# Two blocks of a network on one core: an attention's scale factors turned in halves, a chunk's turns in another order, and a product in quarters

## The reference

```python
def _rwkv7_step(S, inp):
    r, w, k, v, kk, b = inp
    sa = jnp.einsum('bhvk,bhk->bhv', S, kk)
    S = S * w[:, :, None, :] - sa[..., None] * b[:, :, None, :] + v[..., None] * k[:, :, None, :]
    return S, jnp.einsum('bhvk,bhk->bhv', S, r)

# attention, grouped and neighbourhood alike
s = jnp.einsum('bqgrd,bsgd->bgrqs', qi, keys).astype(jnp.float32)   # plus a bias and a mask in the others
p = jax.nn.softmax(s, axis=-1).astype(vals.dtype)
return jnp.einsum('bgrqs,bsgd->bqgrd', p, vals)
```

## Time and profile before

| | |
|---|---|
| median of 3 runs | 4231.01 us (4228.14 to 4231.34) |
| span of the profiled execution | 4224.4 us; the page gives no other time of it |
| PE busy | 3971.7 us, 94% |
| PE weight loads | 2364.7 us, 56% |
| DVE busy | 2271.0 us, 54% |
| ACT busy | 1547.2 us, 37% |
| POOL busy | 763.6 us, 18% |
| L3527, PE, 16704 records | 539.0 us |
| L2720, PE, 3736 records | 171.7 us |
| L3569, PE, 1440 records | 72.5 us |

### The profile page before, as it was taken

How to read it: one execution, slowest core, us unless ns; L and a number is a source line. 1 busy time by engine, 2 the same in 40 slices (tenths; PEclk the granted TensorE clock), 3 DMA queues, 4 the chain that set the end, 5 groups by cost and what they waited for, 6 DMA issues and landing times.

```text
span 4224.4 us, 86296 instructions
## 1 busy us (share of the span) xinstructions
PE 3971.7 (94%) x36672; PEld 2364.7 (56%) x36672; DVE 2271.0 (54%) x3937; ACT 1547.2 (37%) x2591; POOL 763.6 (18%) x953
## 2 busy tenths in 40 slices
PE   8999899899999999999989989899999988998998
PEld 4444875444444444555558876664454437886663
DVE  5773456687343123577544335557678653344556
ACT  2221565200000011233235556663234225556762
POOL 0001311000110000010123332240001114332240
PEclk9999999999999999999999999999999989999999
DMA  4432012344341554344443211222345442222231
GB/s 131 137 111 80 2 71 101 119 145 138 124 155 58 190 184 137 107 170 151 172 140 85 72 53 63 78 82 95 105 162 173 172 150 71 71 60 69 75 103 69
DMA packets 349565, 468.01 MB, mean 111 GB/s; under 512 B 55383, under 2 KB 252791, under 8 KB 348224
## 3 DMA queue, kind: packets, MB, share of 16 engines
q1 hardware_dynamic: 298176, 266.26, 20.5%
q0 software_dynamic: 51008, 196.23, 13.3%
HBM read 328.14 MB, written 147.86 MB: 113 GB/s over the span
## 4 chain that ended last, share of the span: by engine, by line
PE 84%; DVE 6%; ACT 4%; issue 3%; DVEq 1%; DMA 1%; POOL 0%; POOLq 0%; ACTq 0%; SPq 0%
PE psum L492 22%; PE psum L1081 13%; PE psum L708 12%; PE psum L3527 11%; PE psum L2734 5%; PE psum L2750 4%; PE psum L463 3%; PE psum L2720 3%; PE psum L3065 2%; PE psum L2037 1%; ACT arena L2796 1%; PE psum L3569 1%; ACT arena L2817 1%; PE psum L2756 1%; PE psum L433 1%
## 5 line engine op out<-in xcount | busy, mean ns | idle before, releaser
L492 PE MATMUL psum<-arena 128*128 128x512 f32 x2352 | 1030.4, 594 | 8.5 <-DVEq L222 3.6
L492 PEld LDWEIGHTS psum<-arena 128*128 128x128 f32 x2352 | 444.5, 190 | 553.5 <-issue 538.0
L3527 PE MATMUL psum<-arena 64*64 64x64 f32 (+7 forms) x16704 | 539.0, 242 | 58.2 <-issue 33.7
L1081 PE MATMUL psum<-arena 128*128 128x512 f32 x1344 | 583.4, 595 | 9.4 <-DMA arena<-w_down 3.9
L708 PE MATMUL psum<-arena 128*128 128x512 f32 x1232 | 536.7, 596 | 5.9 <-POOLq L222 3.8
L3527 PEld LDWEIGHTS psum<-arena 64*64 64x64 f32 (+2 forms) x16704 | 463.1, 142 | 128.3 <-issue 68.2
L1081 PEld LDWEIGHTS psum<-arena 128*128 128x128 f32 x1344 | 254.6, 191 | 328.3 <-issue 319.2
L708 PEld LDWEIGHTS psum<-arena 128*128 128x128 f32 x1232 | 232.6, 190 | 303.3 <-issue 293.0
L2847 DVE CUSTOM_DVE_ANT_0 arena<-psum,arena 128x512 f32<-128x512 f32 (+3 forms) x532 | 293.4, 591 | 195.1 <-PE psum L2734 189.1
L2796 ACT COPY arena<-psum 128x1024 f32<-128x1024 f32 (+3 forms) x290 | 244.9, 844 | 177.8 <-PE psum L2720 171.6
L2734 PE MATMUL psum<-arena 64*128 64x512 f32 (+3 forms) x1192 | 257.6, 524 | 13.5 <-DVE arena L2847 10.1
(11 more groups left out here) (398 smaller groups left out, 4706.4 us busy)
## 6 DMA issues: line engine op xcount, KB each, us to landing
arena<-w_in SPq DMA_DIRECT2D x86, 512.0 KB, 5.6
proj<-arena SPq DMA_DIRECT2D x172, 256.0 KB, 2.0
arena<-w_mod POOLq DMA_DIRECT2D x24, 1024.0 KB, 5.7
arena<-down_sum SPq DMA_DIRECT2D x40, 512.0 KB, 3.7
arena<-proj POOLq DMA_DIRECT2D x31, 640.0 KB, 5.2
arena<-proj SPq DMA_DIRECT2D x28, 640.0 KB, 7.0
arena<-w_down SPq DMA_DIRECT2D x30, 512.0 KB, 3.8
x_home<-arena POOLq DMA_DIRECT2D x26, 512.0 KB, 3.2
```

Source lines behind the costliest of these rows:

```text
L492: ins = pe.matmul(ps[:, b, :], L[:, k, :], R[:, k, :], start=(p in ("P1", "P5", "P6", "P7") and k == 0), stop=(k == KT // 2 - 1), skip_gro ...
L1081: ins = pe.matmul(self.bank(j, b), self.left(p, j, left, *g)[:, k - g[0], :], R[:, k - k0, :], start=(x in ("P1", "P5", "P6", "P7") and k ...
L3527: return pe.matmul(out, lhsT, rhs, start=first, stop=last, skip_group_check=not (first and last))
```

## The change

Three things change.

In `Attention`, where the last chunk of keys is short, the factors are turned by two transposes of 64 rows that are added to the last turn of exponentials, and ScalarE's copy of that turn takes them along, 128 columns more. The 128x128 transpose falls away for these items. The reciprocal on VectorE moves from the end of a step to its start, and GpSimd's widening goes ahead of the bias of a later item.

In `Rwkv`, the turn `x0` of the next chunk and the turns `tV` and `tK` go ahead of `y5`, in the list and in TensorE's program.

In `Rwkv`, the product of the removal queries with the state is a function of its own, `state_q`, with 24 products of 64 rows and 64 columns, issued between `y1` and `xT0`.

```diff
-        self.pt = [take(2 * self.width) for _ in range(2)]
+        self.pt = [take(2 * self.width + P) for _ in range(2)]
...
+    def carries(self, n):
+        return self.chunks(n)[-1][1] < 512
...
                             ins = halves(out, j * m + x, self.p[n % 3][j][:, at + x * P:at + (x + 1) * P])
+                    if g == self.groups(n) - 1 and self.carries(n):
+                        pe.wait_ge(O.sem, O.at(0, f"w{n}"))
+                        ins = halves(out, 2 * m, self.wide_inv[:, n % 2, :])
...
-                    factors(n - 1)
+                    if not self.carries(n - 1):
+                        factors(n - 1)
...
+                    more = P if g == self.groups(n) - 1 and self.carries(n) else 0
+                    copy(self.pt[n % 2][:, 1024 * g:1024 * g + 2 * w + more], 2 * w + more).then_inc(A.sem, 1)
...
         for n in range(-2, self.N + 2):
+            if self.real(n):
+                dve.wait_ge(A.sem, A.at(0, f"e{n}_1"))
+                if n >= 2:
+                    dve.wait_ge(O.sem, O.at(0, f"w{n - 2}"))
+                dve.reciprocal(self.inv[:, 2 * (n % 2):2 * (n % 2) + 2, :], self.sum[:, 2 * (n % 3):2 * (n % 3) + 2, :]).then_inc(Dv.sem, 1)
...
-        out += later("L0 L1") + mine("y4 xT3") + past("P1") + mine("x4")
-        out += mine("y5 xT4") + past("H", inv) + later("x0") + mine("RB0", rows) + mine("x5 xT5")
-        return out + mine("S2 y6 tV tK tB z")
+        out += later("L0 L1") + mine("y4 xT3") + past("P1") + mine("x4") + later("x0") + mine("tV tK")
+        out += mine("y5 xT4") + past("H", inv) + mine("RB0", rows) + mine("x5 xT5")
+        return out + mine("S2 y6 tB z")
...
+        def state_q(n):
+            pe.wait_ge(Dv.sem, Dv.at(0, f"Hc@{n}"))
+            out = start(f"G@{n}")
+            for i, (d, j) in enumerate(pairs):
+                for c, p in ((0, 0), (1, 1), (1, 0), (0, 1)):
+                    mm(out[HALF[c], p, 64 * i:64 * i + 64], head("Q", d, p, j, n)[:, HALF[c]], sq("Hc", p, 0, i),
+                       first=(i == 0), last=False)
...
+                if n + 1 < NCH and l == 5:
+                    inverse_first(n + 1)
+                if inv and l == 5:
+                    turn(n, "V")
+                    turn(n, "K")
                 if inv:
                     inverse_y(n, l)
+                if state and l == 1:
+                    state_q(n - 1)
+                if inv:
                     inverse_t(n, l - 1)
```

## The result

The kernel after takes 4286.39 us (median of 4 runs, 4283.33 to 4294.88), the kernel before, measured beside it, 4229.58 (4227.28 to 4231.34). The ratio is 1.0140, 95% interval 1.0128 to 1.0152. The forecast was 4241, with 4213 to 4259 for eight in ten: the sign was right, the size was not. The profiled execution has a span of 4281.5 us against 4224.4, so 57.1 us are to be found where the forecast put 10.7.

A forecast was written before the change was run, and what follows sets the result against it. TensorE was taken to bound recurrences and attentions. On the profiled 4224.4 us, +38.7 - 1 (order), -16 (quarters) and -11 (attentions) gave 4235.1; with 6.6 added for the runs' median, stated as 4241, range 4213 to 4259.

The forecast's parts named there:

- the quarters: State's product in the recurrences: 24 products with 64 columns replace twelve with 128, 0.8 us saved a chunk, -16 us.
- the attentions: All attention changes together: shorter transposes and widening wait, less a longer copy and an added wait; -11 us, from -21 to +13.
- the order's term: Recurrences, x0', tV and tK ahead of y5: z 2.15 us late in 18 chunks, +38.7 us.
- steps 1 to 4: One recurrence chunk: x0' waits for Z, copies queue on ScalarE, y6 2.45 us late, 0.36 back, z 2.1 late.
- Nothing between z and the next Z makes that good: Recurrence, from z to the next chunk's Z: none of the order's 2.15 us delay a chunk is recovered.
- 1.57 - 0.78 = 0.8 saved a chunk: State's product: 24 records take 1.57 us, 48 smaller ones 0.78; over 20 state steps -16 us.
- 0 and 1.57: Bounds in us on what the state's product in quarters saves per chunk; 0.8 was taken.
- moving them past xT0 adds no wait: State's product ahead of xT0: needs only Hc and tB's copy, and x1's evacuation wait stays covered; no added time.
- the added wait: Attentions: reciprocal waits for the second exponential, widening stands before the last turn; 0 to +13 us, taken as +1.
- The -12.8 for the transpose that falls away: Attentions: 114 items lose the 128x128 transpose, 0.19 us net each, 0.59 of them on the path: -12.8 us.
- the attentions and the quarters at "nothing": Two rivals: attention gains nothing, 4253 to 4263 us, chance 0.19; quarters are no faster, 4257 us, chance 0.08.
- The rival in which ScalarE's copies don't hold the tail: Recurrence, x0' to z: only TensorE's order counts, z 0.8 us late, 14.4 us in all; total 4217, chance 0.16.

The follow-up runs named there:

- experiment 1: Kernel before with only the new order at level five (x0 of the next chunk, tV and tK ahead of y5): 4264.77 us, ratio 1.0068.
- experiments 7: Kernel before with only tV and tK moved ahead of y5, x0 of the next chunk left behind H: 4217.44 us, ratio 0.9971.
- experiment 8: Kernel before with only x0 of the next chunk moved ahead of y5, tV and tK left behind y6: 4251.21 us, ratio 1.0051.
- experiment 2: Kernel before with only the state's product in quarters, placed between y1 and xT0: 4242.26 us, ratio 1.0024.
- experiment 6: Kernel before with the state's product in quarters, left at the old place behind xT0: 4241.84 us, ratio 1.0025.
- experiment 5: Kernel before with the state's product still in twelve halves, moved between y1 and xT0: 4237.75 us, ratio 1.0017.
- experiment 3: Kernel before with only the attentions' change, half turns in the grouped attentions included: 4237.49 us, ratio 1.0012.
- experiment 4: Kernel before with the attentions' change, but grouped attentions keep the old whole turn, with the reciprocal first in the step: 4214.72 us, ratio 0.9956.
- dense padding: Kernel before with 12 added products (24 records) of the unit matrix between y1 and xT0 in each chunk: 4239.57 us, ratio 1.0024.

## Why the prediction was right or wrong

The forecast was +10.7 us and the kernel lost 57. Two terms failed, the quarters (-16 us) and the attentions (-11 us), and both in their sign. That the kernel came out slower, as forecast, rests on the order's term alone. Alone, the three parts measured +33, +11 and +6 us, 50 together; the other 6 come only with all three at once, and no run here places them.

- **Part 1, steps 1 to 4: right.** x0' at Z + 0.06 (forecast 0.1), xT4's copy at Z + 4.88 (4.9), z at Z + 9.63 (9.4). 2.30 us a chunk against 2.15; 18 x 2.30 = 41.4. Experiment 1 shows it alone (+33 to +35), and experiments 7 and 8 that neither half does it by itself. "Nothing between z and the next Z makes that good" was wrong by 0.35 us a chunk, 6 us (experiment 1): 35 us remain of the 41, close to the sum's 38.7 because the two errors have opposite signs.
- **Part 2, "1.57 - 0.78 = 0.8 saved a chunk" as a saving of time: wrong, and by the runs of single parts the largest miss.** The row became 0.86, so the saving at the place is right. But nothing of it reached the span: -16 us were forecast for the quarters, and alone they cost 11 (experiment 2), or 11 with no bank in the way (experiment 6). The bound of "0 and 1.57" excluded a loss. The step that failed is the one that counts time saved at a place as time saved, without asking whether the next instructions are there: the waits at packet bounds grew from 21.8 us to 45.3 (experiment 6). In the kernel after it is the same: its recurrences are 6.7 us longer than those of experiment 1, where the forecast had them 16 shorter. Before's trace gave little warning: of its 15.2 us of `issue` in layer 1's recurrence, 4.5 are of this kind.
- **Part 2, "moving them past xT0 adds no wait": wrong for the part alone, right for the kernel after.** The step named tB's copy and didn't time it. In the chunk of experiment 2 tB's copy ends 1.4 us after z starts, and xT0, 0.5 us of TensorE, was what covered it; experiment 5 measures +7, with 7.2 us of this wait in its two recurrences. With the new order in place the copy is done in time, and the wait is not there. The prediction didn't give that reason.
- **Part 3, the added wait bounded by 0 to +13 and taken at +1: wrong.** I looked at VectorE's reciprocal and the items' own room, and not at what is queued ahead of the widening on GpSimd. In the grouped attentions that is another stage: TensorE waits 26.1 us for the widening over all attentions, before 3.1. All half turns alone cost 6 us (experiment 3) where 11 were to be gained, and without the grouped ones' the kernel is 23 us faster (experiment 4). The -12.8 for the transpose that falls away isn't borne out either: the three attentions with half turns in experiment 4 gain 0.2 us in sum over 60 items. The grouped attentions gain 6.7 there with the early reciprocal and the old turn, which the sum had at a cost.
- **The sum.** The recurrences missed by +20 (instruction waits, where -16 stood) and the attentions by +29. Some 9 of these 29 stand in experiment 1 too, whose attentions are before's, at a lower granted clock; no run says how much of that is chance. My rivals had the attentions and the quarters at "nothing"; none had either at a loss, so the range ended at 4259. The rival in which ScalarE's copies don't hold the tail is refuted by experiment 1 (+14 was its price, +33 was measured) and by experiment 8 against 1.

What stays open: what gained most of the 17 us of experiment 4; why dense padding costs 8 us and the quarters' waits 23, where both put 24 more records in nearly the same place; the packets' ends shift by a fraction of a microsecond from chunk to chunk, and I didn't find a rule that gives each wait beforehand.

## What to carry to other kernels

When an edit moves the moment at which a helper engine's small result is wanted, list everything that can stand ahead of it in that engine's queue, other stages' DMA issues included. In a dense stretch of short products count work saved on TensorE at nothing, or less, until one run has shown it, and look at when the instruction packets end. Sort the waits that the profile calls `issue` first: one that ends 0.1 us behind another engine's copy is a wait for that copy. Where a list hands out banks, a step moved forward by one is covered by one step less: time the copy that frees its bank.

## What the runs showed of the hardware

- TensorE's instructions came as 16,384-byte packets, one for about 126 of these matmul records, and TensorE went on no sooner than 1.04 us, after a wait mostly 1.2 to 1.6 us, behind the packet's end. From one bound to the next, waits included, TensorE took 2.4 us at the least and about 4.5 as a rule, where 126 records of the 64*64 form at 15 ns each would take 1.9.
- A stall of TensorE costs again behind itself. The granted clock, the last column but two, in four windows of the kernel after around the stall of 6.3 us that ended at 2728.24:

```profile
2716.00:2721.60 5.60, 4.62 (x42) 2.45 (x44) 4.04 (x16) 2.05 (x6) 0.00 (x0) 1.00 0.05 20
...
2728.20:2730.20 2.00, 1.96 (x12) 1.41 (x14) 0.42 (x2) 1.55 (x2) 1.39 (x2) 0.50 0.00 0
2730.20:2732.20 2.00, 2.00 (x8) 0.68 (x4) 0.65 (x2) 1.83 (x4) 0.00 (x0) 0.50 0.00 0
2732.20:2734.20 2.00, 1.44 (x12) 0.60 (x12) 1.67 (x9) 0.00 (x0) 0.00 (x0) 0.95 0.00 0
```

  TensorE ran at 2.4 GHz before the stall, did nothing for 6.3 us, and ran at 1.2 GHz for four microseconds behind it; behind the stall that ended at 2557.47 the granted clock was 0.50 until past 2563.40. The mean of layer 1's attentions, 0.95 with these stalls, is 0.99 in before and in experiment 4, which hasn't got them.
